# Row maxima of two attention groups from 64-row matmuls, the two heads in turn

## What is computed

```
for g, (window, dilation) in enumerate(((128, 1), (512, 4), (2048, 16))):
    ...
    s = jnp.einsum('brhcqe,brhcke->brhcqk', qb, kb) * (E ** -0.5)
    ...
    s = jnp.where(valid, s, -jnp.inf)
    m = jnp.max(s, axis=-1)
    p = jnp.exp(s - m[..., None])
    l = jnp.sum(p, axis=-1)
    o = jnp.einsum('brhcqk,brhcke->brhcqe', p, vb)
...
wts = jnp.exp(ms - jnp.max(ms, axis=0))
den = jnp.sum(wts * jnp.stack(dens), axis=0)
num = jnp.sum(wts[..., None] * jnp.stack(outs), axis=0)
o_b = (num / den[..., None])
```

## Time and profile before

| | us |
|---|---|
| median of 3 runs | 1446.14 |
| lowest, highest | 1445.55, 1446.64 |
| the profiled execution | 1445.83 |
| its span | 1444.1 |
| TensorE (PE) busy in it | 1423.4 (99%) |
| VectorE (DVE) busy | 939.9 (65%) |
| ScalarE (ACT) busy | 650.9 (45%) |

### The profile page before, as it was taken

How to read it: one execution, slowest core, us unless ns; L and a number is a source line. 1 busy time by engine, 2 the same in 40 slices (tenths; PEclk the granted TensorE clock), 3 DMA queues, 4 the chain that set the end, 5 groups by cost and what they waited for, 6 DMA issues and landing times. The chain is left out here.

```text
span 1444.1 us, 21717 instructions
## 1 busy us (share of the span) xinstructions
PE 1423.4 (99%) x7604; PEld 1211.9 (84%) x7604; DVE 939.9 (65%) x1603; ACT 650.9 (45%) x969; POOL 34.9 (2%) x39
## 2 busy tenths in 40 slices
PE   7999999999999999999999999999999999999998
PEld 5888888888888888888888888888888889888987
DVE  7897768686868676778834784467536866544423
ACT  5355546465555555546333453344345356212211
POOL 0200000000000000012100000000000000000000
PEclk9999999999999999999999999999999999999999
DMA  5211121212121212334222212221222233333602
GB/s 205 94 44 59 64 68 59 73 58 73 58 73 51 80 44 79 109 102 110 80 76 59 59 59 85 66 57 55 94 59 59 59 113 116 139 116 118 248 30 88
DMA packets 37495, 120.59 MB, mean 84 GB/s; under 512 B 6248, under 2 KB 6568, under 8 KB 37416
## 3 DMA queue, kind: packets, MB, share of 16 engines
q1 hardware_dynamic: 37424, 119.61, 25.7%
HBM read 84.79 MB, written 22.12 MB: 74 GB/s over the span
## 5 line engine op out<-in xcount | busy, mean ns | idle before, releaser
L822 PE MATMUL z_ps<-h_hi,w_hi 128*128 128x512 f32 x704 | 278.6, 396 | 1.8 <-issue 1.3
L824 PE MATMUL z_ps<-h_hi,w_lo 128*128 128x512 f32 x704 | 274.7, 390 | 0.0
L823 PE MATMUL z_ps<-h_lo,w_hi 128*128 128x512 f32 x704 | 274.4, 390 | 0.0
L822 PEld LDWEIGHTS z_ps<-h_hi,w_hi 128*128 128x128 f32 x704 | 132.4, 188 | 28.4 <-issue 2.9
L824 PEld LDWEIGHTS z_ps<-h_hi,w_lo 128*128 128x128 f32 x704 | 132.1, 188 | 28.3
L823 PEld LDWEIGHTS z_ps<-h_lo,w_hi 128*128 128x128 f32 x704 | 132.3, 188 | 25.2
L1805 DVE TENSOR_TENSOR w_lo<-mix,w_hi 128x512 fp32r<-128x512 f32 x84 | 56.1, 689 | 80.9 <-ACT w_hi L1315 80.6
L1725 DVE TENSOR_TENSOR w_lo<-w_stage,w_hi 128x1024 fp32r<-128x1024 f32 x45 | 55.0, 1223 | 76.7 <-ACT w_hi L1237 76.5
L1498 ACT ACTIVATE pt<-pb 128x512 f32<-128x512 f32 (+1 forms) x80 | 43.4, 543 | 119.5 <-PE pb L1048 119.2
L860 PE MATMUL z_ps<-h_hi,w_hi 128*128 128x512 f32 x224 | 91.5, 408 | 0.0
L862 PE MATMUL z_ps<-h_hi,w_lo 128*128 128x512 f32 x224 | 87.9, 392 | 0.0
(11 more groups left out here) (328 smaller groups left out, 3259.0 us busy)
## 6 DMA issues: line engine op xcount, KB each, us to landing
w_stage<-w_in SPq DMA_DIRECT2D x44, 512.0 KB, 3.6
raw<-w_in SPq DMA_DIRECT2D x44, 512.0 KB, 3.5
z_swap<-zz SPq DMA_DIRECT2D x96, 128.0 KB, 2.3
gate_d<-gate SPq DMA_DIRECT2D x15, 512.0 KB, 3.1
x_in<-x SPq DMA_DIRECT2D x8, 512.0 KB, 8.0
o_a_d<-o_a SPq DMA_DIRECT2D x8, 512.0 KB, 5.1
w_stage<-w_a SPq DMA_DIRECT2D x8, 512.0 KB, 4.2
cos_t<-gate_d SPq DMA_DIRECT2D x8, 512.0 KB, 4.8
```

The lines of the kernel that those rows point to most:

```text
L822: nc.tensor.matmul(z_ps[hf][:], w_hi[s][:, k, :], h_hi[:, k, t], start=k == 0, stop=False)
L823: nc.tensor.matmul(z_ps[hf][:], w_hi[s][:, k, :], h_lo[:, k, t], start=False, stop=False)
L824: last = nc.tensor.matmul(z_ps[hf][:], w_lo[s][:, k, :], h_hi[:, k, t], start=False, stop=k == KT - 1)
```

## The change

The maxima of groups 0 and 1 come from the rounded operands alone: each matmul takes only the 64 rows of its own head of q_two and k_two, and the heads take turns block by block. The waits on the lo parts and on the copies go; in their place stands one on the rounded operands of the group (qk_hi_done). Both heads of a burst now wait together until VectorE has taken both heads of the burst whose bank they write.

```diff
-            def maxima(i, g, m, h):
+            def maxima_of_pair(i, g, m):
 
-                u = 2 * (g * 4 + m) + h
+                u = 2 * (g * 4 + m)
                 if first(i):
                     if u >= 4:
-                        pe.wait_ge(mx_taken, max_count(u - 3))
-                elif u >= 2:
-                    pe.wait_ge(mx_taken, i * N_MAX + max_count(u - 1))
+                        pe.wait_ge(mx_taken, max_count(u - 2))
                 else:
-                    pe.wait_ge(mx_taken, i * N_MAX)
-                pe.wait_ge(qk_lo_done, i * 4 + 2 * g + 2)
-                pe.wait_ge(q_dupped, i * 4 + 2 * g + h + 1)
-                for blk, at, before in max_queries(g, m):
+                    pe.wait_ge(mx_taken, i * N_MAX + max_count(u))
+                pe.wait_ge(qk_hi_done, i * 8 + 4 * g + 4)
+                todo = max_queries(g, m)
+                for blk, at, before in todo:
                     lo = blk - 1 if before else blk
                     at += 0 if before else P
-                    last = nc.tensor.matmul(max_bank(i, g, m)[:, h, at:at + P * (blk + 1 - lo)], q_two[g][h][:, P * blk:P * blk + P],
-                                            k_two[g][h][:, P * lo:P * blk + P], start=True, stop=True)
-                last.then_inc(mx_made, 1)
+                    for h in range(2):
+                        rows = slice(EDIM * h, EDIM * (h + 1))
+                        last = nc.tensor.matmul(max_bank(i, g, m)[:, h, at:at + P * (blk + 1 - lo)], q_two[g][h][rows, P * blk:P * blk + P],
+                                                k_two[g][h][rows, P * lo:P * blk + P], start=True, stop=True)
+                        if blk == todo[-1][0]:
+                            last.then_inc(mx_made, 1)
...
                             else:
-                                for h in range(2):
-                                    maxima(i, g, m, h)
+                                maxima_of_pair(i, g, m)
```

## The result

The changed kernel takes **1449.41 us** (median of 15 runs, 1448.52 to 1450.25); the kernel before took 1446.08 us in as many runs beside it. The ratio is 1.0024, with a 95% interval of 1.0017 to 1.0030: slower by 3.3 us, 0.24%. The forecast was 1449.3. The profiled execution after has a span of 1447.6 us against 1444.1, 3.5 us more; the prediction's sum was 3.25.

The account below looks back on a forecast made before the run. TensorE's stream was taken as the bound. Losses of 0.88 us (first pair), 2 x 0.71 (pairs 1 and 2) and 0.95 (pair 3) made 3.25 us, giving 1449.3 us, 0.22% slower; range 1447.2 to 1451.2, the forecast's own 1448.4 to 1450.2.

Parts of the forecast that it names:

- The bound: Whole kernel: time is the length of TensorE's stream, busy 1423.4 of 1444.1 us; attention-stage waits only 0.5 and 0.2 us.
- One burst: Each clear two-pair burst of maxima: 0.62 us against 0.46 or 0.47, so 0.155 us longer, priced from line 1017.
- The rival of a smaller price: All bursts: height change costs about half of 0.155 us each, about +1.5 us, 1447.7 us; chance 0.20.
- halves of 256 columns might not overlap: Rival, 44 pairs of 256-column matmuls: 0.11 us more each, 4.8 us more, about 1454 us; chance 0.05.
- No drain at all: Rival, ends of bursts: bursts take 2 x 0.11 us instead of 0.46, gaining 7.5 us, 1438.6 us; chance 0.07.
- The pause: First pair, 677.51 us: TensorE's 0.65 us standstill for ACT absorbs the first two bursts' 0.31 us, its end unmoved.
- The first pair: First pair of heads: six bursts outside the pause lose 5 x 0.155 + 0.105 = 0.88 us.
- Pairs 1 to 3: Last three pairs of heads: losses of 0.71, 0.71 and 0.95 us, with late VectorE absorbing part in slots 10 to 14.
- The anchor: Before slot 10's burst: ACT's key copies release VectorE at 830.77 us, so losses in slots 10 and 11 don't move VectorE.
- The rival in which nothing is absorbed: All bursts: VectorE and ACT shift with TensorE, each burst pays in full, 4.8 us, 1450.9 us; chance 0.14.
- The waits, costed at nothing: Attention stage: dropped waits gain nothing; the stricter wait for both heads costs nothing where VectorE is early, late in slots 11, 12, 14.
- The break-even: Burst length: half height begins to gain at about four pairs, 0.84 us against 0.92 at full height.

Follow-up runs that it names:

- the second experiment: The kernel before with the 64-row slice alone, keeping its order of heads and its waits: 1449.54 us, ratio 1.0026 to the kernel before.

## Why the prediction was right, step by step

**The bound.** That TensorE's stream is the time held: the two distances in TensorE's timeline add up to the whole growth of the span, 3.54 of 3.5 us, and other engines' work is unchanged.

**One burst, 0.62 against 0.46.** Measured 0.62 with 256 columns; the price of 0.155, taken from line 1017 by leaving out six pairs, came out as 0.16. Taken instead up to the second projection behind, where the longer record no longer enters, the burst of 256 columns went from 683.77 - 682.84 = 0.93 (the line below, and the earlier trace rows) to 683.98 - 682.89 = 1.09. Two prices that the prediction had taken over or estimated held as well, measured in the same way: 0.15 us behind the scores of the pair before (slot 9 of pair 1, 0.97 against 0.82), and 0.11 in slot 14 of the first pair, with transposes behind it, where it had 0.105. The rival of a smaller price, by which the entry at line 1017 belonged to its three waits, fell: 0.32 us stands at every entry behind a projection, and 0.31 to 0.32 also in the middle of a burst. That halves of 256 columns might not overlap fell with the 0.50 us for four of them. No drain at all fell with the first load behind a burst: the last of four half-height loads that begin at 683.21 and hold for 0.30 together starts at about 683.32 (0.30 less the 0.19 of one), and the full-height load comes at 683.64, 0.32 later.

```profile
683.77 0.40 PE L823 MATMUL z_ps<-h_lo,w_hi 128*128 128x512 f32 x1
```

**The pause.** Its end stood still and the first two bursts' 0.31 us vanished in it, as said.

**The first pair, the term that was mis-sized.** Predicted 0.88 us, measured 1.12. The five bursts followed by projections cost 0.16 and not 0.155, and the rest, 0.2 us, lies outside the bursts, in a term that the prediction has not at all: 0.02 at the pause, and 0.02 to 0.06 in each of five stretches of projections behind a burst. It sits in the first projections of a stretch. Behind the burst of slot 8 the ten steps that follow the second projection take 671.22 to 673.49 before, 2.27 us or 0.227 each, and 671.42 to 673.75 after, 2.33 (the lines below, before and then after), and behind slots 13 and 15 it is the same; from there on the steps are 0.227 in both kernels. Projections behind the full-height bursts of four times 256 columns are slowed in the same way, only for fewer steps. No run here tells why.

```profile
671.22 0.39 PE L823 MATMUL z_ps<-h_lo,w_hi 128*128 128x512 f32 x1
...
673.49 0.39 PE L824 MATMUL z_ps<-h_hi,w_lo 128*128 128x512 f32 x1
...
671.42 0.40 PE L823 MATMUL z_ps<-h_lo,w_hi 128*128 128x512 f32 x1
...
673.75 0.39 PE L824 MATMUL z_ps<-h_hi,w_lo 128*128 128x512 f32 x1
```

**Pairs 1 to 3.** Predicted 0.71, 0.71 and 0.95, 2.37 us in all; measured 0.83, 0.67 and 0.92, 2.42. That the sum is so close is in part luck: the first of the three is 0.12 too small and the others a little too large. The anchor held: VectorE's release moved by 1.42 us, about what TensorE was late by then (1.12, and two bursts), and its finish in slot 12 by 1.43, no more. The next projection is recorded at 845.55 instead of 843.96 and streams 0.10 later, 1.69 in all, so slots 10 to 12 lost 1.69 - 1.42 = 0.27; the prediction had 0.29. In slot 14 TensorE was 1.94 late going in (857.06 against 855.12) and 1.68 at the record of the transposes (857.80 against 856.12); as their two first matmuls hold for 0.44 instead of 0.38 us, they stream 0.06 later, so 1.74 late. That is 0.20 absorbed, and the prediction had 0.20, by a burst that no longer waits: 857.06 to 857.38 is the 0.32 of a clear one. The rival in which nothing is absorbed fell.

**The waits, costed at nothing.** The stricter wait cost little, not nothing: 0.62 us with full height, 0.20 with half height, both by the trace's distances and below what the times can show. The prediction had counted it within slot 12. In both comparisons the order of the heads changes together with the wait, so neither figure is the wait's alone for certain.

**The reading of the order.** The prediction priced height and alternation as one thing, because line 1017 has both, and the expectation of the second experiment made the alternation a condition of the overlap. It is none: with the heads one after the other the bursts are the same. That touched no number of the forecast, since the changed kernel does alternate.

**The break-even.** "At about four pairs", with 0.84 against 0.92: measured 0.85 against 0.92.

## What to carry to other kernels

Price a change of matmul height by the steps it adds between heights, read from a place in the same trace that already makes them: here a step in and out costs some 0.4 us together (the 0.62 us of a burst less 2 x 0.11 for its two pairs). Halves that run side by side lost 0.16 us in a burst of two pairs and won 0.07 in one of four; three were not run, and by the same figures I estimate 0.73 us for them, a little more than the 0.69 of six full-height matmuls. When an engine bounds the kernel, look not only at what a burst costs but at where it stands: moving bursts out of the slots in which their consumer is late gave 2.8 us (2.5 by the trace) without making any matmul cheaper. A wait that appears in the wait list after a change may be an old one that was hidden inside a group of instructions; undo the height, not the wait, to find out.

## What the runs showed of the hardware that was not expected

Matmuls on the lower and the upper 64 rows run as two streams whatever their order in the program: head 0, 0, 1, 1 takes the 0.75 us that 0, 1, 0, 1 takes, and 0, 0, 0, 0, 1, 1 takes 0.99, as long as four of one half. The Trainium skill says both things: "TensorEngine Tiling (Array Packing)", Key Properties, that different tiles can load and multiply in parallel, with which these runs agree; and "TensorE: Matmul & The Clock Gate", Part 3, that matmuls are strict in program order in start and end. By the second, head 1's matmuls in these two orders would have had to begin behind head 0's last, and the 0.75 and 0.99 us say that they did not: in the order 0, 0, 0, 0, 1, 1 the program's last matmul is recorded from 683.57, and head 0's last from 683.79. The signal does not run ahead in the same way. Both heads raise a semaphore with their last matmul, and in that burst the trace has its two events at 684.08 and 684.12 us: neither comes before head 0's last matmul, recorded from 683.79 for 0.28, is through, though head 1's was through earlier by its record. All 32 bursts of that kernel show the same. So here a semaphore on the matmul that stands last in the program would not have come too early for the other half; the kernels of this case raise one for each head all the same.

The step between the heights costs the same 0.31 to 0.32 us from start to start with 256 columns on either side, in both directions, where matmuls of one height follow at 0.115. Behind matmuls of 128 columns it is 0.26.
